# The second attention of a two-block transformer kernel, turned before it is divided, with f32 products that also make the sums

## The reference, cut to what matters

```
s = jnp.einsum('bqhd,bkhd->bhqk', qb, kb).astype(jnp.float32) * scale
mask = jnp.arange(start, end)[:, None] >= jnp.arange(end)[None, :]
s = jnp.where(mask[None, None], s, -jnp.inf)
p = jax.nn.softmax(s, axis=-1).astype(vb.dtype)
outs.append(jnp.einsum('bhqk,bkhd->bqhd', p, vb))
...
o = jnp.concatenate(outs, axis=1).reshape(B, L, N_HEADS * V_HEAD_DIM)
return o @ w_o
```

## Time and profile before

| | us |
|---|---|
| median of 3 runs (2107.93 to 2109.66) | 2108.4 |
| the profiled execution | 2107.83 |
| its span | 2106.0 |
| TensorE busy | 2019.0, 96% |
| second attention, first score product to first product of `wo` | 1029.15 to 1180.59 |

### The profile page before, as it was taken

The page is one execution under the profiler, slowest core; times in us unless marked ns, Lnnn a source line. Parts: engine busy times, 40 slices in busy tenths (PEclk is TensorE's granted clock), DMA queues, the critical chain, the costliest instruction groups (busy, mean ns, idle before and its releaser), DMA issues.

```text
span 2106.0 us, 36640 instructions
## 1 busy us (share of the span) xinstructions
PE 2019.0 (96%) x13714; PEld 1837.9 (87%) x13714; DVE 901.5 (43%) x1726; ACT 845.0 (40%) x1459; POOL 819.6 (39%) x500
## 2 busy tenths in 40 slices
PE   8999999998999999989988999999999989999997
PEld 6887888887877778988777889999999879999997
DVE  6873541128443330167588363343400573333103
ACT  3223433325544442154577444443422453344321
POOL 1445424432434444324533234434344224443441
PEclk7999999998999999989999999999999999999999
DMA  9742003221322322212100013222232112222321
GB/s 362 249 170 80 16 16 99 91 80 41 100 90 87 102 100 101 71 61 101 61 0 0 31 51 100 88 82 86 84 110 91 51 41 90 100 90 80 110 101 40
DMA packets 54952, 184.39 MB, mean 88 GB/s; under 512 B 6992, under 2 KB 10320, under 8 KB 54864
## 3 DMA queue, kind: packets, MB, share of 16 engines
q1 hardware_dynamic: 53024, 180.97, 24.9%
q10 hardware_dynamic: 1840, 2.19, 0.3%
HBM read 181.03 MB, written 2.10 MB: 87 GB/s over the span
## 4 chain that ended last, share of the span: by engine, by line
PE 89%; DVE 7%; ACT 2%; issue 2%; DMA 1%; DVEq 0%; ACTq 0%; SPq 0%
PE PS L713 70%; PE PS L922 2%; PE PS L1001 2%; PE PS L828 2%; PE PS L880 2%; DVE work L2777 1%; PE PS L792 1%; PE PS L955 1%; DVE ada_acc L2321 1%; PE PS L1260 1%; PE PS L897 1%; PE PS L819 1%; PE PS L1081 1%; PE PS L1069 1%; PE PS L1417 1%
## 5 line engine op out<-in xcount | busy, mean ns | idle before, releaser
L1463 POOL TENSOR_TENSOR w_lo<-w_raw,w_hi 128x1024 fp32r<-128x1024 f32 x263 | 637.8, 2433 | 953.5 <-ACT w_hi L1619 953.4
L1619 ACT ACTIVATE w_hi<-w_raw 128x1024 fp32r<-128x1024 f32 (+2 forms) x307 | 295.4, 982 | 724.9 <-PE PS L713 671.8
L713 PE MATMUL PS<-H_hi,w_lo 128*128 128x256 f32 (+3 forms) x2088 | 561.8, 320 | 20.6 <-DVE H_lo L2724 8.0
L713 PE MATMUL PS<-H_lo,w_hi 128*128 128x256 f32 (+3 forms) x2088 | 554.6, 317 | 0.0
L713 PE MATMUL PS<-H_hi,w_hi 128*128 128x256 f32 (+3 forms) x2088 | 553.6, 316 | 0.0
L713 PEld LDWEIGHTS PS<-H_hi,w_lo 128*128 128x128 f32 x2088 | 351.9, 190 | 59.3 <-issue 13.6
L2777 DVE SCALAR_TENSOR_TENSOR work<-PS,vec,work 128x512 f32<-128x512 f32 (+4 forms) x264 | 187.0, 751 | 442.9 <-ACT work L1916 433.3
L713 PEld LDWEIGHTS PS<-H_hi,w_hi 128*128 128x128 f32 x2088 | 352.3, 191 | 25.8
L713 PEld LDWEIGHTS PS<-H_lo,w_hi 128*128 128x128 f32 x2088 | 352.4, 191 | 24.6
L713 PE MATMUL PS<-mid_hi,w_lo 128*128 128x256 f32 (+2 forms) x968 | 228.6, 294 | 3.6 <-DVE work L2777 3.6
L713 PE MATMUL PS<-mid_hi,w_hi 128*128 128x256 f32 (+2 forms) x968 | 226.9, 292 | 0.0
(11 more groups left out here) (374 smaller groups left out, 3028.9 us busy)
## 6 DMA issues: line engine op xcount, KB each, us to landing
w_raw<-stream SPq DMA_DIRECT2D x289, 512.0 KB, 3.2
ada_w<-ada SPq DMA_DIRECT2D x48, 512.0 KB, 6.2
X<-xT SPq DMA_DIRECT2D x8, 256.0 KB, 5.2
yT<-X SPq DMA_DIRECT2D x16, 128.0 KB, 1.7
rel_raw<-rel ACTq DMA_DIRECT2D x4, 256.0 KB, 2.7
vec<-vecs ACTq DMA_DIRECT2D x1, 390.0 KB, 3.7
sin_t<-rope ACTq DMA_DIRECT2D x1, 264.0 KB, 2.9
cos_t<-rope ACTq DMA_DIRECT2D x1, 132.0 KB, 2.6
```

What stands on the lines that cost most here:

```text
L713: last = pe.matmul(out[:, c0 + a:c0 + b], w, x[:, a:b], start=start and i == 0, stop=stop and i == 2)
L1463: gp.tensor_tensor(w_lo[:, o], w_raw[:, o], w_hi[:, o].bitcast(F32), ALU.subtract)\
L1619: return act_.activation(out, in_, ACT.Copy, scale=scale)
```

## The change

The second attention is written anew. Its five tiles and ten steps stay.

- The exponentials are turned over as they are. `normalize` and the accumulated sums go. `turn_over` of tile t waits for the exponential alone.
- The turned exponentials go out of PSUM by one plain copy in f32: that of a head's first tile by ScalarE, the four others by VectorE. The buffer `PT2` is double, one half for each `par`.
- The product with v is one f32 product in place of three f32r ones. Its weights are 128 columns: 64 columns of v and 64 ones, so that the sums come out in the other 64 rows of PSUM. `V2` holds them for all heads; it is written once, when v is made. `stage_head` of v, its lower part, and the four fills with zeros go.
- ScalarE makes the reciprocal as exp(-ln(sum)) (`turn_sums`), in two pieces per head; VectorE multiplies both halves by it (`take_out`: half the sum times r, twice the output times r); GpSimd finishes a pair with a Newton step (`finish_o2`: a product and a difference), ScalarE rounds (`round_o`), GpSimd makes the lower part (`lower_o2`).
- Score products are cut at a PSUM bank: 128, 256, 384 and 512 columns in one, where there were pieces of 256. The late product is spread over four steps, one piece each. `wo` waits pair by pair and no longer for all of them. In the second head of a pair the 528-key tile comes before the 512-key one.
- TensorE's ten steps are unrolled over all pairs; the other engines keep a loop.

```diff
-                def turn_over(p, w):
-                    pe.wait_ge(pn_ok, p * U + (w + 1))
-                    pe.wait_ge(pt_lo, p * U + (w + 1))
+                def turn_over(p, t):
+                    i, q0, qn, ke, c0 = tile2(t)
+                    pe.wait_ge(p_ok, p * U + (t + 3))
+                    wait_turned(t - 2 if t >= 2 else t - 2 + U, p if t >= 2 else p - 1)
...
-                        for n_, (l, r) in enumerate(((v2_lo, sh), (v2_hi, sl), (v2_hi, sh))):
+                def product(p, par, late, j, stop):
+                    return pe.matmul(o_psum2(par, late)[:, a - a0:b - a0], v_weights2(p, par, j), pt2(par, j, a, b),
+                                     start=j == 0, stop=stop, skip_group_check=True)
+                def outputs_early(p, par):
+                    wait_turned(par * 5, p)
+                    wait_turned(par * 5 + 1, p)
+                    if p + par:
+                        pe.wait_ge(o_ok, part2(p, par, 0, 1) + 2)
+                    product(p, par, 0, 0, False)
+                    product(p, par, 0, 1, True).then_inc(pv_done, 1)
...
+            def finish_o2(p):
+                gp.wait_ge(o_ok, part2(p, 1, 1) + 2)
+                gp.wait_ge(o_hi, p + 1)
+                gp.tensor_tensor(half2, half2, twice2, ALU.mult).then_inc(two_ok, 1)
+                gp.wait_ge(two_ok, p + 1)
+                gp.tensor_tensor(O2[:, :], twice2, half2, ALU.subtract).then_inc(fin_ok, 1)
+            with gp.Fori(1, H2 // 2 - 1) as p:
+                lower_qk2(p + 1, 0)
+                finish_o2(p - 1)
+                lower_qk2(p + 1, 1)
+                lower_o2(p - 1)
...
+                def turn_sums(p, par, late, first=False):
+                    act_.wait_ge(pv_done, part2(p, par, late))
+                    act_.activation(r, o_psum2(par, late, 1), ACT.Ln).then_inc(ln_ok, 1)
+                    act_.wait_ge(ln_ok, part2(p, par, late))
+                    act_.activation(r, r, ACT.Exp, scale=-1.0).then_inc(inv_ok, 1)
...
                 def step(p, t, first, last):
-                    par, i = divmod(t, nq)
+                    par, pos = divmod(t, 5)
+                    if pos == 1:
+                        weights(p, t - 1, first)
                     exps(p, t)
+                    if pos == 0 and not first:
+                        turn_sums(p - 1, par, 1)
+                    if pos == 2 and not (first and par == 0):
+                        turn_sums(*before2(p, par), 0, first)
+                    if t == 9 and not first:
+                        round_o(p - 1)
...
-                    v.tensor_scalar(pb, pb, r, None, ALU.mult).then_inc(pn_ok, 1)
+                def take_out(p, par, late, first=False):
+                    v.wait_ge(inv_ok, part2(p, par, late))
+                    v.scalar_tensor_tensor(o_part2(half2, par, late), o_psum2(par, late, 1), 0.5, r, ALU.mult, ALU.mult)
+                    v.scalar_tensor_tensor(o_part2(twice2, par, late), o_psum2(par, late, 0), 2.0, r, ALU.mult,
+                                           ALU.mult).then_inc(o_ok, 1)
```

More of the change, by code:

```diff
@@ L520, in end, with over_pairs @@
                 self.base, self.k, self.g = self.base + turns * self.per, 0, None
-        def over_pairs(eng, pairs, U, step, chain=None, per=0):
-            for t in range(LEAD):
+        def over_pairs(eng, pairs, U, step):
+            for t in range(U):
                 step(0, t, True, False)
[L527 to L537, removed]
+            with eng.Fori(1, pairs - 1) as p:
+                for t in range(U):
+                    step(p, t, False, False)
+            for t in range(U):
                 step(pairs - 1, t, False, True)
@@ L719, in begin, with batch @@
                 pe.wait_ge(free[(BATCH[name][batch][2] + i) % 4], free_before(name, batch, i, g) + 1)
-            def batch(name, bi, g, n, blocks, tiles, kks, cols, x, T, h_ready=None, between=None):
+            def batch(name, bi, g, n, blocks, tiles, kks, cols, x, T, h_ready=None, between=None, place=None):
                 done = 0
@@ L731, in batch @@
                             begin(name, bi, m, g)
+                            if place is not None:
+                                place(m)
                         for k in range(kk):
@@ L929, in step @@
[L929 to L939, removed]
-                    elif i < 2 and not first:
-                        outputs(p - 1, 1, True, i)
+                def product(p, par, late, j, stop):
+                    a, b = (256 if late else 0), (S2 if late else 256)
+                    a0 = a
+                    a = max(a, TILES2[j][0])
+                    return pe.matmul(o_psum2(par, late)[:, a - a0:b - a0], v_weights2(p, par, j), pt2(par, j, a, b),
+                                     start=j == 0, stop=stop, skip_group_check=True)
@@ L950, in _ @@
+                for pos in range(4):
+                    outputs_late(pairs - 1, 1, pos)
             pe.wait_ge(set_up, 1)
@@ new lines, in step @@
+                    if pos >= 3 and not last:
+                        if pos == 3:
+                            act_.wait_ge(s_full, p * U + (par * 5 + 5))
+                        stage_head(p + 1, par, pos - 3)
+                    if t == 9 and not first:
+                        round_o(p - 1)
+                act_.sem_inc(o_hi, 1)
+                over_pairs(act_, pairs, U, step)
+                p = pairs - 1
+                turn_sums(p, 0, 1)
+                turn_sums(p, 1, 0)
+                turn_sums(p, 1, 1)
@@ L1906, in ffn @@
+                round_o(p)
             def ffn(up, down, T, layer, mid0, behind_first=None, behind_up=None):
@@ L2559, in step @@
+                def step(p, t, first, last):
+                    par, pos = divmod(t, 5)
+                    if pos >= 2:
+                        weights(p, t - 1, first)
+                    elif pos == 0 and par:
+                        weights(p, t - 1, first)
+                    elif pos == 0 and not first:
                         weights(p - 1, U - 1)
```

318 lines of the change are left out of this document (151 added, 167 removed).

## The result

After: 2120.99 us (2120.45 to 2122.03); before, on the same chip: 2108.16. The ratio is 1.006, interval 1.0043 to 1.0077: slower by 0.6%. The prediction of 2092 and its range, 2075 to 2105, were wrong, in sign too. The span went from 2106.0 to 2119.7.

The account below looks back on a forecast made before the run. TensorE, busy 96% of the span, was taken to bound the kernel, with the chain setting the changed stage's beat. 2107.83 less 13.2 (pairs) and 2.8 (ends) is 2091.8, median 0.6 above, so 2092; range 2075 to 2105.

Parts of the forecast that it names:

- TensorE's work: Second attention: output product from 2.5 to 1.25 us a head, scores 2.85 to 2.65, all work 7.3 to about 5.85.
- the forecast gain of 13.2: Second attention: a pair of heads takes 16.3 us against 17.96; 1.65 x 8 = 13.2 us less.
- the walk: Timing one head of the second attention through its steps: 7.86 and 8.02 us, plus 0.44, making 16.3 a pair.
- Rival 4: f32 products cost twice the rows' spacing; first late piece and early product add 0.33 each a head: 2102; 2 in 100.
- A head step by step: Second attention, engine waits followed from step 0 to 4: 8.02 us a head with 2.2 of TensorE waiting.
- TensorE's wait at a head's second step: Step 1 waits 0.83 us for the second exponential, behind ScalarE's copy of the head's first turned tile.
- my own price: Output product in the second attention: f32 of 256 columns at 0.216 us, 1.25 us a head in all.
- the wait of B: Theory from the experiments: VectorE's early take-out waits for GpSimd's Newton step, since half2 and twice2 are one buffer.
- some 6: VectorE in the second attention: about 6.6 us of durations a head, some 6 with their overlap.
- Rival 3: TensorE's clock falls inside the stage, 1.5 us a stretch: once a pair 2104 (5 in 100), twice 2116 (4 in 100).
- Its dear form, 2116: Clock falls twice a pair in the second attention: 24 us, 2116, slower than before; 4 in 100.
- The ends: Start and end of the second attention stage, 7.7 us together before: 2.8 off, bounds nothing and 5.

Follow-up runs that it names:

- e7: Changed kernel plus idle bf16 products: 12 behind a head's first transpose, 16 ahead of the early product of a pair's second head; 2117.24 us, ratio 1.0039.
- e1: Changed kernel with each f32 output product run as two f32r products of rounded operands, lower parts left out; 2119.98 us, ratio 1.0051.
- e2: Changed kernel with own half and twice buffers for each pair, VectorE's and GpSimd's loops unrolled; 2108.82 us, ratio 1.000.
- e5: e2 with one f32r product in place of each f32 output product, lower parts left out; 2103.45 us, ratio 0.9976.
- e9: e5 plus 14 idle bf16 products after the single transpose of each head but the first; 2103.12 us, ratio 0.998.
- e4: Changed kernel with the transposes ahead of the output product in each of TensorE's ten steps; 2096.56 us, ratio 0.9942.
- e6: Changed kernel with both own buffers for each pair and transposes ahead of the output products; 2087.67 us, ratio 0.9897.

## Why the prediction was wrong

| | clean pair | beat | time |
|---|---|---|---|
| after | 19.85 | 20.27 | 2120.99 |
| e7, idle products | 19.85 | 19.82 | 2117.24 |
| e1, f32r twice | 18.92 | 20.55 | 2119.98 |
| e2, own buffers | 18.85 | 18.81 | 2108.82 |
| e5, f32r once, own buffers | none | 19.0 | 2103.45 |
| e9, the same with idle products | 17.4 | 18.5 | 2103.12 |
| e4, transposes first | 16.8 | 17.25 | 2096.56 |
| e6, both | 16.2 | 16.16 | 2087.67 |

**"TensorE's work": the price of an f32 product failed.** I read "f32 of 256 columns 1.73/8 = 0.216" from the earlier trace rows and took x8 for eight products. They were four. The trace shows a true f32 product as two matmul instructions: every group of L938 has an even count, and a head's seven products make fourteen. A product of 256 columns is 0.43 us, and a head's take 3.1 us where I had 1.25. My sum had 2.5 for before; read in the same way, from start to start, before's took some 2.9 (1.25 of it for the nine from 1104.18). That was not a cheaper product, but a dearer one. On the path that is the early product (0.72 for 0.34) and the late one with the 16-row piece (1.02 for 0.33), 1.1 a head, 2.2 a pair, **17 us**. By itself this undoes the forecast gain of 13.2. The 17 is worked out on the walk. The runs bear out most of it: e1 gave back 0.93 us a pair for products 0.94 shorter on the path, e9 against e2 1.42 (18.85 less 17.43) for products 1.9 shorter, 11 us in eight pairs, because the waits of 0.71 and 0.49 for exponentials then show. The rule of the Trainium skill (FP8 and Floating Point Precision, TensorE Precision Notes: true FP32 takes four passes) that I set aside for the rows was right. An estimate by it, four times the 0.12 of an f32r product of 256 columns, is 0.48, and the trace has 0.43. The count of instructions would have settled it beforehand. The program issues 160 products at L828, in the first attention of the kernel before, and its trace has

```profile
L828 PE MATMUL PS<-V_all,PT 128*128 128x128 f32 x320 | 42.7, 280 | 0.7 <-ACT PT L1619 0.7
```

Rival 4 held the mechanism, "twice the rows' spacing", with 2 chances in 100. It had 0.33 each for the two on the path, where they gained 0.38 and 0.69, so its 2102 was too low too.

**"A head step by step": a wait was left out.** I had GpSimd, "which can begin the Newton step at 4.79 and needs two operations of 1.33", and held it against ScalarE's rounding alone. VectorE's early take-out writes the same buffer and waits for the same end: in my numbers it would have begun at 7.45 in place of 6.42, and TensorE's wait of 0.24 would have been 1.27. Measured: 1.38, in one head of each pair. e2 gives 1.0 a pair back, **8 us**, and 12 with the clock.

**The rest of the walk** was nearly right. TensorE's wait at a head's second step is 1.03 from the transpose's spacing (1110.67 + 0.12 to 1111.82), where I had 0.83: a signal took 0.33 and not 0.20, and the copy 0.28. With both heads that makes 16.3 + 2.2 + 1.05 + 0.4 = 19.95 against 19.85. But at about my own price e9's clean pair, without the wait of B, takes 17.4 and not 16.3: some 1 us a pair, 8 us, I can place only in part (0.4 as above); with the 3.1 us of f32 products this rest does not show beside them. Nearly all of it lies ahead of a head's second step: from the start of step 0 to that of step 1 e9 takes 2.35 (1119.97 to 1122.32) and 2.70, where the walk has 2.13 and 1.97. Its late product with the 16-row piece takes 0.53 (1120.64 to 1121.17) and not 0.33, its early one 0.25 and not 0.34; that is 0.2 more a pair, and some 0.5 stays unplaced. The take-outs at 0.42 to 0.45, logarithm 0.38 to 0.39 and exponential 0.41 to 0.43 cost what I took or less, and VectorE's 5.9 us a head is my "some 6".

**What I missed in the walk** is that its waits came from the order of two steps and not from the rest of the change. I wrote "fuller gaps than before, made by the new order", and took them as given. The gaps of one step and the work of the same step stood side by side: e4, one line moved, is worth 24 us, more than the price or the buffer.

**Rival 3, the clock**, had the right price for one stretch and too high a one for two. A stretch of 3.4 us cost 1.5 (the pair of 21.35), the others 0.6 each. There are three in six pairs, not one or two a pair; together they cost 2.7 us, at that rate some 3.5 in eight. Its dear form, 2116, came nearer to the result than any other number of the prediction, but for a cause that is worth those 3.5. Where the work is thinner (e1, e5, e9) they cost 9 to 13: eight times the beat less the clean pair. The Trainium skill (TensorE: Matmul & The Clock Gate, A second HAM failure mode) describes swings between half and full clock in a kernel whose TensorE idles briefly and often between groups of matmuls. After and e7 agree with it, three swings and, with the waits filled, none; but the kernel before waits three times a head too and kept its clock, so the rule does not tell these kernels apart. Whether transposes count for less, as its section on PE-mode transpose says, no run here tests. TensorE's busy time does not tell them apart either: e2 kept the clock with 17.0 of 20 us busy, and e4, with 17.2 and 18.1 in its windows at 1.00, lost it twice in its six pairs and again at the end.

**The ends**: 2.9 us against 7.7, where I took 2.8 off: 4.8, near the far end of my bound. It is so although the last products ran partly at the lower clock, behind a wait of 2.63:

```profile
1188.32 0.96 PE L938 MATMUL PS<-PT,V 128*128 128x256 f32 x4 [2.63 <-DVE work L2587]
...
1192.14 2.66 PE L938 MATMUL PS<-PT,V 128*128 128x272 f32 x6
1194.43 0.81 PE L742 MATMUL PS<-OK_hi,w_lo 128*128 128x272 f32 x2
```

**Sum.** From 2092: price 17, the take-out's wait 8, the clock 3.5, the copy and signals 3, the ends -2: 2121.5, against 2120.99. So the two steps that failed are the price, 17 us of 29, and the wait that was left out, 8. The 8 and the 3.5 rest on runs; of the 17, 11 do and the rest on the walk; the 3 is read from one head. Since terms that are on the walk can hide behind one another, that the sum comes out within 1 us is in part luck.

Not settled: what keeps the clock in e2 and loses it in e5 and e9 (a wait's length, or what lies between two of them), and the 0.5 us a pair that the walk lacks at the assumed price.

## What to carry to other kernels

Before a price is read from a run "x8", hold the count of instructions of that line against the products that the program issues; where a rule and a row differ by a factor of two, this is the first thing to look at. For each buffer that a moved step writes, list who must be done with it, not only for the engine that looks critical. And where a walk through the steps finds an engine waiting and then working on what nobody waits for, try the two the other way round before pricing anything else: here that alone took the kernel from 0.6% slower to 0.6% faster, and with the buffer to 1% faster.

## What the runs showed of the hardware

- A true f32 product stands in the trace as two matmul instructions of 0.216 us each at 256 columns (0.12 at 128), where one of f32r of 256 columns takes 0.12: 320 for 160 products at L828 of before, 224 for 112 at L938 of after. Transposes of f32 data are one instruction each (160 for 160 at L819 of before).
- The first f32r product behind a bf16 one or behind an f32 transpose takes longer than the next: in e1 two of 272 columns take 0.33 rather than 0.24, in e9 one takes 0.21 (1123.11 to 1123.32) rather than 0.12, and in after a score product of 256 columns 0.22 (1105.89 to 1106.11) and the next 0.12. Why, no run here tests.
- Less work on TensorE can cost its clock. With own buffers and f32r products the six pairs spent some 41 of 114 us at 1.2 GHz (e5), with own buffers and f32 products none (e2), and with the transposes first as well none (e6): 2103, 2109 and 2088 us. After spent 10 of 122 there.
